# Two mixing branches moved into the stream of one projection, phase by phase, and dummy products at the norms

## The reference

```python
h = rmsnorm(x, norm1_g)
z = h @ w_in                      # RWKV columns | mLSTM columns | 8 input/forget gates | 2 x 1024 gates
y_rw = rwkv7(z_rw)                # 8 heads of 64; token shift, decay, state over 256 tokens, group norm
y_ml = mlstm(z_ml)                # 4 heads of 128; causal conv of 4 taps, stabilised gates, state, layer norm
merged = sigmoid(g_rw + b) * (y_rw @ p_rw) + sigmoid(g_ml + b) * (y_ml @ p_ml)
x = x + merged @ w_out            # then the expert layer (peer) and a last norm
```

## Time and profile before

| | before |
|---|---|
| median of 3 runs | 2564.57 us |
| profiled execution, its own time | 2560.37 us |
| its span, first to last instruction | 2558.6 us |
| mean granted TensorE clock | 0.942 |
| TensorE, VectorE, ScalarE busy | 2291.9, 1655.9, 1033.0 us |
| HBM read | 358.02 MB |

### The profile page before, as it was taken

One profiled execution on the slowest core, in us unless ns is written; L12 is line 12 of the kernel. 1 busy time (PEld: TensorE's weight loads), 2 busy tenths in 40 slices (PEclk: granted clock), 3 DMA queues, 4 the chain that ended last, 5 costly groups with the idle time before them and its releaser, 6 DMA issues. The chain is left out here.

```text
span 2558.6 us, 46152 instructions
## 1 busy us (share of the span) xinstructions
PE 2291.9 (90%) x18078; PEld 2149.6 (84%) x18078; DVE 1655.9 (65%) x3044; ACT 1033.0 (40%) x1674; POOL 110.4 (4%) x42
## 2 busy tenths in 40 slices
PE   7999999999999989996993734778999999999997
PEld 7997889998998878996993723778999999788886
DVE  5654666656655667654546555548988995677775
ACT  5443455444443455442332121233444444333333
POOL 0000000000000000000000000006910000000000
PEclk9999999999999989998995965889999999999999
DMA  5553434553553424552540000344544445555564
GB/s 190 174 191 113 162 114 151 182 179 124 174 191 124 142 85 156 188 199 71 184 158 14 3 1 0 124 141 132 168 143 139 140 141 180 172 191 191 189 190 138
DMA packets 99156, 361.43 MB, mean 141 GB/s; under 512 B 11168, under 2 KB 14896, under 8 KB 98864
## 3 DMA queue, kind: packets, MB, share of 16 engines
q1 hardware_dynamic: 98992, 359.11, 43.4%
HBM read 358.02 MB, written 1.05 MB: 140 GB/s over the span
## 5 line engine op out<-in xcount | busy, mean ns | idle before, releaser
L1034 DVE TENSOR_TENSOR w_lo<-ring,w_hi 128x1024 fp32r<-128x1024 f32 (+1 forms) x304 | 397.5, 1308 | 245.0 <-ACT w_hi L851 244.8
L594 PE MATMUL ps<-x_hi,w_hi 128*128 128x272 f32 (+1 forms) x1664 | 490.7, 295 | 31.3 <-DVE w_lo L1034 16.7
L851 ACT ACTIVATE w_hi<-ring 128x1024 fp32r<-128x1024 f32 (+1 forms) x304 | 341.2, 1124 | 404.5 <-PE ps L594 362.3
L594 PE MATMUL ps<-x_hi,w_lo 128*128 128x272 f32 (+1 forms) x1664 | 481.8, 290 | 0.0
L594 PE MATMUL ps<-x_lo,w_hi 128*128 128x272 f32 (+1 forms) x1664 | 479.8, 288 | 0.0
L594 PEld LDWEIGHTS ps<-x_hi,w_hi 128*128 128x128 f32 x1664 | 316.2, 190 | 38.0 <-DVE x_lo L1057 15.2
L594 PEld LDWEIGHTS ps<-x_lo,w_hi 128*128 128x128 f32 x1664 | 316.5, 190 | 1.0
L594 PEld LDWEIGHTS ps<-x_hi,w_lo 128*128 128x128 f32 x1664 | 316.6, 190 | 0.0
L234 ACT ACTIVATE v_gated_hi<-ring 128x1024 fp32r<-128x1024 f32 x128 | 135.8, 1061 | 217.8 <-PE ps L2437 217.0
L2224 PE MATMUL ps<-tok_hi,u_mid_hi 128*128 128x256 f32 x736 | 213.6, 290 | 1.2 <-POOL u_mid_lo L240 1.2
L2224 PE MATMUL ps<-tok_hi,u_mid_lo 128*128 128x256 f32 x736 | 208.1, 283 | 0.0
(11 more groups left out here) (475 smaller groups left out, 5079.1 us busy)
## 6 DMA issues: line engine op xcount, KB each, us to landing
ring<-in_gate_up SPq DMA_DIRECT2D x176, 512.0 KB, 3.6
ring<-in_peer_v SPq DMA_DIRECT2D x128, 512.0 KB, 3.5
ring<-in_peer_u_mid SPq DMA_DIRECT2D x92, 512.0 KB, 3.6
ring<-in_down SPq DMA_DIRECT2D x64, 704.0 KB, 4.0
ring<-in_w_in SPq DMA_DIRECT2D x46, 512.0 KB, 3.5
ring<-in_peer_u_early SPq DMA_DIRECT2D x36, 512.0 KB, 3.9
ring<-in_na_qk SPq DMA_DIRECT2D x16, 512.0 KB, 3.6
ring<-in_da_qk SPq DMA_DIRECT2D x16, 512.0 KB, 3.7
```

The lines of the kernel that those rows point to most:

```text
L594: mm = nc.tensor.matmul(ps[:, bank, 0:ntok], parts[left][:, slot, t * P:(t + 1) * P], rhs[right][:, k, 0:ntok], start=start and n == 0, st ...
L851: A.activation(parts[0][:, n % SLOTS, 0:width[n]], ring[:, n % SLOTS, 0:width[n]], ACT.Copy).then_inc(hi_done.sem, 1)
L1034: V.tensor_tensor(parts[1][:, n % SLOTS, 0:width[n]], ring[:, n % SLOTS, 0:width[n]], parts[0][:, n % SLOTS, 0:width[n]].bitcast(F32), ALU ...
```

## The change

There are three parts.

1. **One program for `w_in` and both branches.** `mixers` replaces the stages from the norm to the split. Each engine runs over 47 slots. In a slot it first does its share of one `w_in` tile (TensorE the 24 products, ScalarE the high part of the tile three ahead, VectorE the eviction and the residual three ahead), and then the phases that the table `PHASES` puts there, in its order. The columns come in the order `W_IN_ORDER`, so that the low-rank inputs of RWKV arrive first. The tokens are split before the norm, and the norm's factor is applied at the eviction, as in the first block. The token shift and the convolution are made tile by tile. The key's norm is taken on 8 partitions instead of 128. Group norm's weight, bias and gate are applied after the results are turned. The results leave as high and low parts, so the copy and the split ahead of `p_rw` go.
2. **mLSTM on 128 partitions.** Two heads of a chunk stand on the two halves of the partitions, so its element-wise operations have half as many elements in the free dimension.
3. **Dummy products.** `keep_busy` issues 20 fp32 products of `ones` with itself (128x128) into PSUM bank 7 at the end of the first three SwiGLUs and of both attentions. Nothing reads them.

To have enough semaphores, those of the first block are cleared and freed at its end, with one more barrier of all engines.

```diff
+                for _ in range(20):
+                    nc.tensor.matmul(ps[:, 7, 0:P], ones[:, :], ones[:, :], start=True, stop=True)
+                if n < 3:
+                    keep_busy()
+                pe.wait_ge(taken, taken0 + 3)
+                keep_busy()
+    nc.clear_and_free_semaphores(own)
+    nc.all_engine_barrier()
-            linear("w_in", x_parts, KD, SEQ, 4, lambda m, bank: V.tensor_copy(z[:, m, :], ps[:, bank, 0:SEQ]), norm)
-        save("z", z[:, :, :])
-        rwkv(nc, a, env, z, row, masks, y_rw)
-        save("y_rw", y_rw[:, :, :])
+        y_rw, y_ml, gates = mixers(nc, a, env, branches)
-                    link = Chain(dve, v_step)
-                    V.tensor_copy(both[:, 0:4, :], y_rw[:, :, :])
-                    link(V.tensor_copy(both[:, 4:8, :], y_ml[:, :, :]))
-            split(both, y_parts, SEQ)
-            linear("p_rw", [part[:, 0:4, :] for part in y_parts], 4, SEQ, 4, lambda m, bank: V.tensor_tensor(merged[:, m, :], ps[:, bank, 0:SEQ], z[:, 30 + m, :], ALU.mult))
+            linear("p_rw", y_rw, 4, SEQ, 4, lambda m, bank: V.tensor_tensor(merged[:, m, :], ps[:, bank, 0:SEQ], gates[:, m, :], ALU.mult))
...
+W_IN_ORDER = [12, 13, 4, 5, 6, 7, 0, 1, 2, 3] + list(range(8, 12)) + list(range(14, Z_TILES))
+N_SPLIT = 3
+PHASES = {2: ["lora"], 6: ["kk_sum"], 7: ["kk_root"], 8: ["kk"], 9: ["decay"], 10: ["hats_b"], 11: ["hats_k"], 12: ["hats_r"],
+          14: ["turn", "bonus"], 15: ["prod 0"], 16: ["prod 1"], 17: ["prod 2"], 18: ["prod 3"],
+          22: ["silu"], 23: ["if_in"], 24: ["if_cum"], 25: ["if_wide"], 26: ["if_max"], 27: ["if_exp"],
+          28: ["v_turn"], 29: ["k_turn"],
+          31: ["rec 0 0"], 32: ["rec 0 1"], 33: ["rec 0 2"], 34: ["rec 1 0"], 35: ["rec 1 1"], 36: ["rec 1 2"],
+          37: ["rec 2 0"], 38: ["rec 2 1"], 39: ["rec 2 2"], 40: ["rec 3 0"], 41: ["rec 3 1"], 42: ["rec 3 2"],
+          30: ["scores"], 43: ["gn_mean"], 44: ["gn_var"], 45: ["gn_back"]}
+for _n in range(11):
+    PHASES.setdefault(19 + _n, []).insert(0, f"inv {_n}")
+for _slot, _name in ((31, "s_turn"), (32, "k_weigh"), (33, "state 0"), (34, "state 1"), (35, "state 2"), (36, "mix 0"), (37, "mix 1"),
+                     (38, "mix 2"), (39, "mix 3"), (40, "ln_mean"), (41, "ln_var"), (42, "ln_back"), (39, "gates 0 9"), (46, "rw_out"),
+                     (46, "ml_out"), (46, "gates 9 16")):
+    PHASES.setdefault(_slot, []).append(_name)
+N_SLOTS = 47
...
+            def tile(slot):
+                pe.wait_ge(lo_done.sem, w.first + slot + 1)
+                pe.wait_ge(taken, slot - 1)
+                for k in range(KD):
+                    mm = products(slot, k, slot % 2)
+                mm.then_inc(used, 1)
...
+            def kk_sum():
+                pe.wait_ge(s["kk_sq"], 1)
+                pe.wait_ge(s["lora_kept"], 1)
+                for m in range(4):
+                    mm = nc.tensor.matmul(ps[0:8, 2, 0:SEQ], ind[:, m, :], sqk[:, m, :], start=(m == 0), stop=(m == 3))
+                mm.then_inc(s["kk_sum"], 1)
+            def kk_wide():
+                pe.wait_ge(s["kk_inv"], 1)
+                for m in range(4):
+                    mm = nc.tensor.matmul(ps[:, 3 + m // 2, 256 * (m % 2):256 * (m % 2) + 256], ind_t[:, m, :], norm8[:, :], start=True, stop=True)
+                mm.then_inc(s["kk_wide"], 1)
...
+            def inv_step(n):
+                if n >= 1:
+                    _lv, pair = step_of(n - 1)
+                    pe.wait_ge(s["t1_kept"], n)
+                    if n >= 2:
+                        pe.wait_ge(s["added"], n - 1)
+                    for ch in (2 * pair, 2 * pair + 1):
+                        for m, half, mc in heads():
+                            nc.tensor.matmul(ps[half, 4 + ch % 2, mc], inverse[half, ch, 1, mc], t1[half, ch, mc], start=True, stop=True)
+                        for m, half, mc in heads():
+                            mm = nc.tensor.matmul(ps[half, 4 + ch % 2, 256 + CH * m:256 + CH * m + CH], t1[half, ch, mc], inverse[half, ch, 1, mc],
+                                                  start=True, stop=True)
+                    mm.then_inc(s["xx_ready"], 1)
+                if n < 10:
+                    _lv, pair = step_of(n)
+                    pe.wait_ge(s["level_ready"], n + 1)
+                    if n >= 2:
+                        pe.wait_ge(s["added"], n - 1)
+                    else:
+                        pe.wait_ge(s["inv_begun"], 4)
+                    for ch in (2 * pair, 2 * pair + 1):
+                        for m, half, mc in heads():
+                            mm = nc.tensor.matmul(ps[half, 2 + pair, 256 * (ch % 2) + CH * m:256 * (ch % 2) + CH * m + CH], level_l[half, ch, mc],
+                                                  inverse[half, ch, 0, mc], start=True, stop=True)
+                    mm.then_inc(s["t1_ready"], 1)
...
+        def act_program(act):
+            link = Chain(act, Tally(link_a))
+            def split_hi(n):
+                if n >= w.n:
+                    return
+                act.wait_ge(ring_full[n % SLOTS].sem, 16 * (w.fills_before[n % SLOTS] + n // SLOTS + 1))
+                if n >= N_SPLIT:
+                    act.wait_ge(used, n - N_SPLIT + 1)
+                A.activation(parts[0][:, n % N_SPLIT, :], ring[:, n % SLOTS, 0:D], ACT.Copy).then_inc(hi_done.sem, 1)
+            def tile(slot):
+                split_hi(slot + N_SPLIT)
+                b = slot % 3
+                if slot < RW_TILES:
+                    act.wait_ge(taken, slot + 1)
+                    if slot >= 2:
+                        act.wait_ge(zs_done, slot - 1)
+                    A.activation(zt[:, slot % 2, :], zb[:, b, 4:260], ACT.Copy, scale=one_less[:, tile_mu(slot):tile_mu(slot) + 1]).then_inc(shifted, 1)
+                elif slot < RW_TILES + 8:
+                    i = slot - RW_TILES
+                    key, m = divmod(i, 4)
...
+            def lora():
+                act.wait_ge(zs_done, 2)
+                act.wait_ge(consts_in, 16 * 9)
+                A.activation(tanh_w[:, :], zs[0:64, 0, :], ACT.Tanh)
+                A.activation(sig_g[:, :], zs[:, 1, :], ACT.Sigmoid).then_inc(s["lora_in"], 1)
+                act.wait_ge(s["lora_out"], 1)
+                for m in range(4):
+                    half = slice(256 * (m % 2), 256 * (m % 2) + 256)
+                    A.activation(sig[:, m, :], ps[:, 2 + m // 2, half], ACT.Sigmoid, bias=col("w0", m))
+                    A.activation(a_gate[:, m, :], ps[:, 4 + m // 2, half], ACT.Sigmoid, bias=col("a0", m))
+                act.wait_ge(s["lora_out"], 2)
+                A.activation(g_f[:, :, :].rearrange("p m t -> p (m t)"), ps[:, 6:8, :].rearrange("p b t -> p (b t)"), ACT.Copy).then_inc(s["lora_kept"], 1)
...
+            def split_lo(n):
+                if n >= w.n:
+                    return
+                dve.wait_ge(hi_done.sem, w.first + n + 1)
+                V.tensor_tensor(parts[1][:, n % N_SPLIT, :], ring[:, n % SLOTS, 0:D], parts[0][:, n % N_SPLIT, :].bitcast(F32),
+                                ALU.subtract).then_inc(lo_done.sem, 1)
+            def tile(slot):
+                b = slot % 3
+                dve.wait_ge(used, slot + 1)
+                src = ps[:, slot if slot < 3 else slot % 2, 0:SEQ]
+                if slot < RW_TILES + 8:
+                    if slot >= 3:
+                        dve.wait_ge(shifted, min(slot - 2, RW_TILES))
+                        dve.wait_ge(zs_done, min(slot - 2, RW_TILES))
+                    if slot >= RW_TILES + 3:
+                        dve.wait_ge(conv_done, slot - RW_TILES - 2)
+                    V.tensor_tensor(zb[:, b, 4:260], src, inv[:, :], ALU.mult).then_inc(taken, 1)
...
+                if 1 <= slot <= RW_TILES:
+                    shift(slot - 1)
+                if RW_TILES + 1 <= slot <= RW_TILES + 8:
+                    taps(slot - 1)
+            def shift(slot):
+                b, i = slot % 3, tile_mu(slot)
+                dve.wait_ge(shifted, slot + 1)
+                V.scalar_tensor_tensor(out=zs[:, slot, :], in0=zb[:, b, 3:259], scalar=col("mu", i), in1=zt[:, slot % 2, :],
+                                       op0=ALU.mult, op1=ALU.add).then_inc(zs_done, 1)
...
+            def inv_step(n):
+                if n == 0:
+                    take_level(0)
+                if n >= 1:
+                    _lv, pair = step_of(n - 1)
+                    dve.wait_ge(s["xx_ready"], n)
+                    two = inverse[:, 2 * pair:2 * pair + 2, :, :].rearrange("p c a k -> p c (a k)")
+                    V.tensor_tensor(two, two, ps[:, 4:6, :], ALU.add).then_inc(s["added"], 1)
+                    dve.wait_ge(s["added"], n)
+                if n + 1 < 10:
+                    take_level(n + 1)
...
+            def local(ch):
+                if ch == 0:
+                    dve.wait_ge(s["inv_begun"], 4)
+                    link(V.memset(ml_state[:, 0:MH, :], 0.0))
+                dve.wait_ge(s["local"], ch + 1)
```

(14 more changed lines are left out.)

1474 lines of the change are left out of this document (821 added, 653 removed).

## The result

| | before | after |
|---|---|---|
| median of 4 runs, us | 2563.7 (2561.8 to 2565.4) | 2450.4 (2447.8 to 2451.2) |
| ratio, 95% interval | | 0.9557 (0.9540 to 0.9573) |
| span of the profiled execution | 2558.6 | 2449.4 |
| last new tokens of the first block end | 1182.74 | 1175.34 |
| from there to the first `p_rw` product | 419.8 | 318.9 |

The forecast was 2450 (2423 to 2490).

The account below looks back on a forecast made before the run. Before, a chain through all engines, bounded by none; merged, TensorE sets the pace. 36.5 + 218.3 + 36.5 + 15.3 + 8 gives 315 against 419.8; 105 plus 10 off 2560.4 gives 2445, median 2450 (2423 to 2490).

Parts of the forecast that it names:

- dummies: First block: twenty dummy products at each of five boundaries keep the clock at 1.00, saving 10 us.
- head, to the start of tile 3: Merged stage, from the first block's last new tokens through the low-rank products to tile 3: 36.5 us.
- TensorE's work at full clock from there: From tile 3 on: 43 w_in tiles at 2.88 us, 123.8, plus 94.5 for the branches' products: 218.3 us.
- waits behind tile 3, without the clock's part: TensorE waiting on same-slot work of VectorE or ScalarE: 31.9 us; the prediction's 36.5 also held half-clock losses.
- half clock and handovers: Merged stage: 4.6 us of half clock behind long gaps, plus 8 (0 to 40) for handovers and table loads.
- tail: From RWKV's last turning to p_rw: finishing both branches, last sigmoids, a barrier and one item's split, 15.3 us.
- the stretch: From the first block's last new tokens to the first p_rw product: 315 us, against 419.8 before.
- lora: RWKV's low-rank products in slot 2: TensorE waits 9 us before them and comes back at half clock.
- Table loads: ScalarE's eleven loads cost 1.28 us each without a drain; with the skill's 1.38 us drain, some 2465.
- TensorE without stalls: Merged stage: VectorE runs far enough ahead that the 36.5 us of stalls go, 2405 to 2435; 17%.
- Coupling: Merged stage: in-order engines let a late phase delay the next residual and tile, 2468 to 2498; 24%.
- The clock inside the stage: Merged stage: short bursts and waits in two PSUM banks drop TensorE to half clock, 2655; 2%.

Follow-up runs that it names:

- the runs that separate them: Changed kernel without the five groups of dummy products: 2462.2 us; kernel before with only those dummies added: 2552.5 us.
- The run with the tile ahead: Changed kernel with TensorE doing the products of tile s+1, instead of tile s, before the phases of slot s: 2426.3 us.
- the run with the phases behind them: Changed kernel with every phase from slot 19 on moved 27 slots back, behind the last w_in tile: 2464.1 us.
- the run with filled waits: Changed kernel with dummy products added in five waits of the merged stage: 2441.3 us.

## Why the prediction was right, by its steps

| step | forecast | measured |
|---|---|---|
| dummies | 10 | 9 and 11 in the runs that separate them |
| head, to the start of tile 3 | 36.5 | 40.6 |
| TensorE's work at full clock from there | 218.3 | 219.2 |
| waits behind tile 3, without the clock's part | 31.9 | 30.9 |
| half clock and handovers | 4.6 + 8 | 14.7, all half clock |
| tail | 15.3 | 13.4 |
| the stretch | 315 | 318.9 |

*The number.* That 2450.4 lies on 2450 to half a microsecond is luck. By the profiled pair 109.2 us went, and 115 were forecast: 3.9 of the difference lie in the stretch and 2.6 in the first block, and 1.0 came back behind them. The 4.2 us by which the first profiled execution lay under its median made up for most of it, since the second one lies 0.8 above its own. The terms are what was right, each to a few us.

*Work.* TensorE is busy for 233.9 us from the start of tile 3 to its last product. Windows of 2 us give its busy time at half clock, and half of that, 14.7 us, is what the clock cost. 219.2 are left. The counts of products and the prices of the earlier trace rows were enough. (The price of 0.43 us for 256 columns does not follow from the earlier trace rows, where two products of 272 columns stand with 1.37 us, not 0.9; the row's length has the end of the last product in it. At 5 us in the sum this did no harm.)

*Waits.* Forecast and measured, in us: "lora" 9 and 10.3; slot 6 3.6 and 4.6; slot 8 1.0 and 2.2; slots 13 and 14 8.1 and 10.0 (1.9 forecast for the eviction and 6.2 for the shift, 5.0 and 5.0 measured); slot 19 6.7 and 4.9; the gates in 24 and 25 3.7 and 4.0; the last chunks and group norm 5.5 and 4.7; small ones 3.3 and 0.5. All of over 1 us were named, by counting what stands ahead of a phase on its releasing engine. Single ones are off by up to 3.1 us, and their sum by 1.0: some of that closeness is luck. The run with the tile ahead shows that this is their cause: it changes only what TensorE does meanwhile.

*Head.* The sums end 21.6 us after the last new tokens (20.3 forecast), and the low-rank products take 8.8 us at half clock through, not 6.5. This is the one term that was too small by more than 3 us.

*The clock.* I gave it up to 2 us behind three of the long gaps. It fell at eight places behind tile 3. Seven of them stand in a wait of TensorE or up to 3 us behind one; the eighth has no wait for 30 us ahead of it. Rows of the changed kernel, around the gate's columns in slot 23:

```profile
1347.45 1.10 PE L1697 MATMUL ps<-w_if,h 128*64 128x4 f32 x32
```

```profile
1342.00:1348.00 6.00, 6.00 (x189) 5.83 (x186) 3.12 (x4) 1.29 (x2) 0.00 (x0) 1.00 0.27 93
1348.00:1353.00 5.00, 5.00 (x47) 4.97 (x44) 0.51 (x3) 3.19 (x5) 0.00 (x0) 0.66 0.00 0
```

TensorE counts as busy for all of both windows; ahead of the fall it did 64 products of 4 columns (128 records, 1343.7 to 1348.5). The same fall stands in all eleven kernels with the merged stage, in these 64 products or within 0.5 us of their end, and lasts for 3.4 us in six of them and longer in the others. The prediction has no term for it, nor for any fall without a wait. The friction of 8 us that I added for handovers stood in the right place of the sum under the wrong name: waits and busy time fill the window, and the handovers cost nothing that the profile shows.

*Table loads.* In the head one of ScalarE's loads starts 0.02 us after the activation before it, and the next activation starts 0.01 us after the load, much as in the earlier trace rows:

```profile
1203.22 0.51 ACT L1865 ACTIVATE zt<-zb,one_less 128x256 f32<-128x256 f32 x1 [0.55 <-DVE zb L2085]
1203.75 1.28 ACT L1879 ACT_TABLE_LOAD   x1
1205.04 0.42 ACT L1879 ACTIVATE tanh_w<-zs 64x256 f32<-64x256 f32 x1
```

The drain of 1.38 us per load of the Trainium skill ("ScalarE: Activation LUTs", What ACT_TABLE_LOAD costs) does not show here either, and the time by it, some 2465, did not come.

*The rivals.* TensorE without stalls: no, the stalls are there. Coupling: no, the waits came to 30.9 us and not to half as much again or double, and the tile ahead, which by that rival would make VectorE late with its residuals, gained all the same. The clock inside the stage: its mean is 0.94 from tile 3 on, far from 0.66. That clock does go back and forth while two PSUM banks are cycled, as the Trainium skill has it ("TensorE: Matmul & The Clock Gate", A second HAM failure mode: psum-queue depth-cycling), but bare tiles in the same two banks, in the run with the phases behind them, stand 2.88 us apart at 1.00; here the falls go with the phases.

*What the prediction did not need and had no answer to* is why the stretch was shorter. My picture, tiles filling the waits of a chain, is worth 11.9 us for the second half of the stage. More came from the two branches filling each other's waits (33.2), and most from the rest (55.8): shorter operations and stages that went, with RWKV's first part among the tiles, which no run takes out. The sum was right because it was counted from below, product by product, and not as a share of the waits saved.

## What to carry to other kernels

Count the work of the engine that will be the bound, and add for each phase what stands ahead of its releaser in the same slot: that gave the stage within 4 us of 319. If such waits are left, let the bounding engine run one unit ahead of its phases; two changed lines gave 24 us. Before two things are merged, ask which of them fills whose waits: here two latency chains side by side gave more (33 us) than the wide products put between them afterwards (12). Dummy products pay in a long wait between stages of dense products (10 us for five), but in the stage of small products half of what they gave by tile 23 was gone at its end (10.8 and 5.6 us), and on top of the tile ahead all of it: there the half clock stood longer further on.

## What was not expected of the hardware

- In three executions whose merged stages differ by nothing but four copies of VectorE in slots 20 to 23 (the changed kernel, the one without dummies, the one with more copies) the half clock stands at the same nine places from the low-rank products to slot 25, to about 3 us; it follows the program. The one with the copies has one more, just ahead of the tail. With everything from slot 3 on the same, a shift of 2.3 us in when TensorE reaches the inversion came with 17 us at half clock in two places, instead of 7.
- It falls in stretches in which TensorE counts as busy all the time: in the 64 products of 4 columns or right behind them, in all eleven kernels, and in the run with filled waits for 10.2 us at the last chunks, 1.3 us behind a wait of 2.9. What the chip goes by was not settled.
- A copy of 128x256 within SBUF takes 0.27 to 0.28 us on VectorE, and such copies start 0.20 us apart, where an eviction of that size takes 0.42.
- The first block has the same instructions in ten of the kernels with dummies, and its end lies up to 3 us apart from one to another. What the rest of the program has to do with this was not looked into.
